# Orders and waits in the seven-product turns of an up projection

## The reference, cut to what matters

```python
D_MODEL = 1024; SEQ = 512; D_FF = 2816; CONV_WIDTH = 3

def conv_ffn(h, w_up, conv_w, conv_b, w_down):
    L = h.shape[1]
    u = h @ w_up
    up = jnp.pad(u, ((0, 0), (CONV_WIDTH - 1, 0), (0, 0)))
    u = conv_b + sum(conv_w[j] * up[:, j:j + L] for j in range(CONV_WIDTH))
    gate, val = jnp.split(u, 2, axis=-1)
    return (jax.nn.silu(gate) * val) @ w_down
```

## Time and profile before

| | us |
|---|---|
| median of 3 runs | 1957.24 (1954.73 to 1957.75) |
| the profiled execution | 1957.02 |
| its span, first to last instruction | 1955.2 |
| PE busy in it | 1913.8 |

### The profile page before, as it was taken

One profiled execution on the slowest core, in us unless ns is written; L12 is line 12 of the kernel. 1 busy time (PEld: TensorE's weight loads), 2 busy tenths in 40 slices (PEclk: granted clock), 3 DMA queues, 4 the chain that ended last, 5 costly groups with the idle time before them and its releaser, 6 DMA issues. The chain is left out here.

```text
span 1955.2 us, 35674 instructions
## 1 busy us (share of the span) xinstructions
PE 1913.8 (98%) x13706; PEld 1764.1 (90%) x13706; DVE 1241.8 (64%) x1875; ACT 973.8 (50%) x1650; POOL 994.9 (51%) x591
## 2 busy tenths in 40 slices
PE   8999999999999999999999999999999999999997
PEld 6887888889889998999877889999999889999997
DVE  6964550215898795066577368998940778988802
ACT  3334442323646673245577545666632454666522
POOL 2535424443467764515656426767543236676642
PEclk9999999999999999999999999999999999999999
DMA  8943002322257753313200114687433115676321
GB/s 335 345 150 97 12 12 86 97 90 72 76 128 186 190 154 108 108 44 109 98 1 1 34 54 119 155 192 174 129 98 108 44 33 122 173 193 161 130 91 51
DMA packets 129894, 222.99 MB, mean 114 GB/s; under 512 B 8145, under 2 KB 97489, under 8 KB 129745
## 3 DMA queue, kind: packets, MB, share of 16 engines
q1 hardware_dynamic: 102560, 193.55, 29.9%
q0 software_dynamic: 25344, 25.17, 8.4%
q10 hardware_dynamic: 1840, 2.19, 0.4%
HBM read 218.78 MB, written 2.10 MB: 113 GB/s over the span
## 5 line engine op out<-in xcount | busy, mean ns | idle before, releaser
L1988 POOL TENSOR_TENSOR w_lo<-w_raw,w_hi 128x1024 fp32r<-128x1024 f32 x167 | 422.2, 2534 | 510.6 <-ACT w_hi L2270 472.8
L2270 ACT ACTIVATE w_hi<-w_raw 128x1024 fp32r<-128x1024 f32 (+2 forms) x299 | 290.4, 982 | 463.5 <-PE PS L1022 385.7
L2131 POOL TENSOR_TENSOR w_lo<-w_raw,w_hi 128x1024 fp32r<-128x1024 f32 x96 | 258.9, 2753 | 140.0 <-ACT w_hi L2270 97.8
L1022 PE MATMUL PS<-mid_hi,w_lo 128*128 128x256 f32 (+2 forms) x968 | 229.1, 294 | 0.2
L1022 PE MATMUL PS<-mid_hi,w_hi 128*128 128x256 f32 (+2 forms) x968 | 226.8, 292 | 0.0
L1022 PE MATMUL PS<-mid_lo,w_hi 128*128 128x256 f32 (+2 forms) x968 | 226.7, 292 | 0.0
L1847 PE MATMUL PS<-D_hi,w_lo 128*128 128x256 f32 (+2 forms) x768 | 216.8, 282 | 4.8 <-DVE w_lo L3707 4.3
L1847 PE MATMUL PS<-D_hi,w_hi 128*128 128x256 f32 (+2 forms) x768 | 216.8, 282 | 0.0
L1847 PE MATMUL PS<-D_lo,w_hi 128*128 128x256 f32 (+2 forms) x768 | 216.7, 282 | 0.0
L1022 PE MATMUL PS<-H_hi,w_lo 128*128 128x512 f32 (+3 forms) x672 | 204.5, 339 | 4.0 <-DVE work L3607 3.7
L1022 PE MATMUL PS<-H_lo,w_hi 128*128 128x512 f32 (+3 forms) x672 | 203.4, 337 | 0.0
(11 more groups left out here) (464 smaller groups left out, 4717.9 us busy)
## 6 DMA issues: line engine op xcount, KB each, us to landing
w_raw<-stream SPq DMA_DIRECT2D x289, 512.0 KB, 3.5
ada_w<-ada SPq DMA_DIRECT2D x48, 512.0 KB, 6.8
w_raw<-stream POOLq DMA_DIRECT2D x24, 512.0 KB, 8.9
w_s<-stream SPq DMA_DIRECT2D x12, 512.0 KB, 5.3
w_s<-stream POOLq DMA_DIRECT2D x12, 512.0 KB, 6.2
w_s_odd<-stream SPq DMA_DIRECT2D x12, 512.0 KB, 5.3
w_s_odd<-stream POOLq DMA_DIRECT2D x12, 512.0 KB, 6.3
X<-xT SPq DMA_DIRECT2D x8, 256.0 KB, 5.4
```

Of the source, the lines that this page charges most:

```text
L1022: last = pe.matmul(out[:, c0 + a:c0 + b], w, x[:, a:b], start=start and i == 0, stop=stop and i == 2)
L1988: gp.tensor_tensor(w_lo[:, o], w_raw[:, o], w_hi[:, o].bitcast(F32), ALU.subtract)\
L2131: gp.tensor_tensor(t.part(w_lo, q), t.src(f, p), t.part(w_hi, q).bitcast(F32), ALU.subtract)\
L2270: return act_.activation(out, in_, ACT.Copy, scale=scale)
```

## The change

GpSimd gives up two waits in turns 1 to 7 and keeps them in turn 0. In turn 0 it takes the lowering of D4 out of the run of D5, D7 and puts it behind lower 4, makes lower 4 wait for VectorE's lower 3, and D4's for sum4. ScalarE rounds product 3 of turn 0 ahead of the two SiLU of classic turn 2. VectorE in up_a makes the fourth sum of activations behind classic turn 1's taps and gates in place of ahead of them; in all stages the sign flip comes behind lower 2, and the two gates of classic turn 2 behind lower 5 of turn 0.

```diff
@@ GpSimd, lower_turns
-                for d in range(1, 4):
+                for d in (1, 2):
                     lower_operand(t, d)
                 for f in range(FAST):
                     if f + 1 < FAST:
                         add_sums(t, f + 1, 1)
+                    if f == 0:
+                        t.wait_lo(gp, 0, 3)
                     fast_lower(t, f, 4)
-                    if f:
+                    if f == 0:
+                        t.wait_s2(gp, 0, 1)
+                        lower_operand(t, 3)
+                    else:
                         if f == FAST - 1:
                             t.wait_lo(gp, f, 3)
                         gated(t, CLASSIC + f - 1, 0)
-                    t.wait_lo(gp, f, 5)
+                    if f == 0:
+                        t.wait_lo(gp, f, 5)
                     fast_lower(t, f, 6)
                     if f + 1 < FAST:
                         add_sums(t, f + 1, 3)
                         fast_lower(t, f + 1, 0)
-                        t.wait_s2(gp, f + 1, 0)
+                        if f == 0:
+                            t.wait_s2(gp, f + 1, 0)
                         fast_lower(t, f + 1, 1)
@@ ScalarE, ffn
-                take(2, psum)
+                take(2, psum, lambda: fast_upper(t, 0, 3))
...
-                    fast_upper(t, f, 3)
+                    if f:
+                        fast_upper(t, f, 3)
@@ VectorE, ffn
-                for k in range(0, KD, 2):
-                    whole(k)
+                whole(0)
+                whole(2)
+                whole(4)
+                if t.l:
+                    whole(6)
+                body(1, psum)
                 if t.l == 0:
-                    signs()
-                body(1, psum)
+                    whole(6)
                 operands()
                 sum2(0)
                 fast_lower(0, 2)
-                if t.l:
-                    signs()
+                signs()
                 taps(2, 0, lambda m: lambda a, b: psum(m)[:, a:b])
                 taps(2, 1, lambda m: lambda a, b: psum(m)[:, a:b])
-                gated(2, 0)
-                gated(2, 1)
...
                     fast_lower(f, 5)
                     if f:
                         v.wait_ge(mid_ok, t.mid0 + 2 * (g - 1) + 1)
-                        gated(g - 1, 1)
+                    else:
+                        gated(2, 0)
+                    gated(g - 1, 1)
```

## The result

| | before | changed |
|---|---|---|
| median | 1955.99 us (4 runs) | 2000.39 us (4 runs, 1993.79 to 2003.35) |
| profiled execution | 1957.02 us | 1998.31 us |
| its span | 1955.2 us | 1996.5 us |
| PE busy | 1913.8 us | 1932.4 us |

A forecast was written before the change was run, and what follows sets the result against it. TensorE was taken to bound the kernel (busy 1913.8 of 1955.2 us), until VectorE's circle of 22.5 us exceeds PE's turn of 20.49. Net 11.5 (up_b) + 10.6 (up_c) + 0 (up_a) = 22.1 on 1957.0 gives 1979.1 us, range 1972 to 1988.

The forecast's parts named there:

- The wait for sum2 hardly binds: GpSimd's wait for sum2: 7.0 us in 6 times, three of them in the first turns, which keep the wait.
- I take 0, between -2 and +4: up_a: VectorE's circle comes to 19.8 us, PE's own pace; the first late join eats the first turn's gain.
- The prediction's own sign for a time above 1990: Above 1990 us, either up_a has joined in or the down stage starts late.
- up_b and up_c: +11.5 and +10.6: Each stage: +1.4 us at the first half product, then five longer VectorE circles, +10.1 in up_b and +9.2 in up_c.
- 51 of 54 meetings: GpSimd arriving during a VectorE instruction with another right behind went next this often; so lower 6 precedes the gate.
- rival 2: Lower 6 beats the gate in some turns alone: 1966 us if half are lost, about 1959 a quarter; chance 0.08.
- the forecast had 3.5 to 4: up_b and up_c, turns 1 to 6: sum2 takes 3.5 to 4 us, held behind GpSimd's add and lower 0.
- joins aren't 22 us apart: Expected sign in turns 1 to 6 of up_b and up_c: VectorE's joins come 22 us apart.
- The first turns: 3.6 to 5.5 us: New orders in the first turns of all three up stages win 3.6 to 5.5 us, if nothing follows.
- The price of the held gate: up_b and up_c: VectorE's gate takes about 2.9 us instead of 0.70 behind lower 6; join 2.2 us later.
- The rule weighed in the prediction: Skill's rule: two-SBUF-input VectorE instructions contend only with GpSimd's SBUF reads, by issue order; sum2 would go during descriptor writing.
- the 0.1 us that the forecast reckoned with: Later turns: without its wait lower 6 comes 0.1 us before the gate is issued, and so goes first.

## Why the prediction was wrong

The direction and the place were right: slower, by PE's wait for the join in the middle of product 6, behind a sum2 held by GpSimd. The time was 21 us too low, and the steps failed as follows.

- **"The wait for sum2 hardly binds."** This is the step that failed most. Its 7.0 us of idle time were read as what it costs GpSimd, and so as what its loss could change. But the wait kept lower 1 away while sum2 was waiting. Without it sum2 takes 6.2 to 6.9 us in place of 4.5 to 4.6. Its loss alone costs 18.7 us on the median (4 to 22 in single executions); in the profiled one nearly all of it lies in up_a (179.5 in place of 160.0).
- **up_a: "I take 0, between -2 and +4."** It became 21.2 us longer (182.7 against 161.5). The sum there used 4.63 us for the held sum2 and ended at PE's own pace, with nothing to spare; 2.2 us more of lower 1 became a stop in each of turns 1 to 6. The prediction's own sign for a time above 1990, that up_a has joined in, is what came.
- **The clock** wasn't in the sum: 18.8 of the 41.3 us in the profile. The rows of before gave no sign of it, since the stops in them had no half clock behind them.
- **up_b and up_c: +11.5 and +10.6.** Measured are +10.6 and +10.2, but by another way, and that the sums agree is chance. The order at the gate was taken from 51 of 54 meetings, as lower 6's in every turn; in turns 1 to 6 lower 6 came 0.14 to 0.36 us ahead of the gate's issue in all 12 cases and won 6, as in rival 2. In these six turns sum2 takes 6.2 to 6.3 us (the forecast had 3.5 to 4), since lower 1 holds it as well; PE stops for 2.0 to 3.4 us, and the half clock comes on top. In the six between, sum2 takes 2.3 to 3.1 us and PE doesn't stop. So joins aren't 22 us apart in each turn.
- **The first turns: 3.6 to 5.5 us.** Right as measured alone (5.45). In the changed kernel it is worth nothing that four runs each could show (2000.4 with the new orders, 1999.6 with the old ones). The forecast had allowed for part of it.
- **The price of the held gate** was right: 2.90 us, where the forecast had "about 2.9". With the wait for lower 5 alone given up the whole costs 12.5 us (1963.11 less 1950.59), about half of the forecast's 22.1 plus 5.5, and PE stops in six of the twelve turns 1 to 6 of up_b and up_c. The two waits' costs alone, 12.5 and 18.7, don't add up to the 49.8 us of both (2000.39 less 1950.59); by the stages of the profiled executions most of the rest lies in up_b and up_c, where both losses hold the same sum2 (6.2 to 6.3 us, against 3.9 to 4.4 behind a held gate with the wait for sum2 kept).
- **The rule weighed in the prediction.** The Trainium skill (SBUF — State Buffer, section "Who interferes with whom") lets issue order decide who blocks. Here it didn't: sum2, issued at 619.27, was waiting before the first of the two lowerings was issued at 619.84, and both went ahead of it. The measurement decides.

What stays open is why lower 6 or the gate goes first. The traces show what goes with it. In the six kernels without the wait for lower 5, in up_b and up_c, behind a lower 5 that wasn't itself held, the gate went first in all 26 meetings in which lower 6 was issued 145 ns or less ahead of it; lower 6 went first in all 18 with 149 ns or more; in the 12 between, either did. So with the 0.1 us that the forecast reckoned with, the gate would have gone first. It is no rule for other meetings: in up_a, behind a lower 5 that was itself held, lower 6 went first with as little as 25 ns.

Open as well is which stops are followed by half clock: a stop of 3.3 us in up_c of the run with the waits alone wasn't, and the one ahead of classic turn 2 of up_a, 2.4 to 3.7 us long in all ten traces, was in two of them.

## What to carry to other kernels

A wait by which one of two engines that exclude each other stands aside is an opening for the other. Its price isn't its idle time: before it is given up, write down which instructions of that engine will then stand in a row, and reckon with an instruction of the other engine that waits for all of them. And a stop of TensorE that looks small in a sum may cost nearly its own length again in granted clock (1.71 us behind stops of about 2 us here), so a change that lets VectorE pass PE's pace by a little can lose twice.

## What the runs showed of the hardware

- A VectorE instruction with both inputs in SBUF that was waiting while a GpSimd instruction ran didn't get in ahead of GpSimd's next one where that was issued 0.5 us before the end of the first: it waited through both in all 69 such cases of the ten traces (sum2 6.2 to 6.9 us, ending 1.09 after the second lowering in the row shown), and a tap of 0.48 us through three (6.60). Where GpSimd's next instruction was issued less than 0.1 us before that end, or later because GpSimd itself waited, VectorE went in between.
- Stops of 2.0 to 3.4 us in the seven-product turns were followed, from 0.4 us before to 1.3 us after their end, by some 3.4 us at 1.2 GHz in 11 of 12 cases of the changed kernel and in 5 of 5 with the wait for lower 5 kept: about 1.71 us lost each time. In all ten traces half clock came with 35 of 41 stops of 1.9 us or more in these turns (it began between 1.6 us before and 1.5 us after their end), and with 1 of 23 stops of 1.0 to 1.9 us. Where PE was given other matmuls ahead of the wait, it wasn't so in up_a and up_c.
